# A two-block float32 model on one core: late projection tiles of the mixers in three split products, and another order of work in the first blocks

## The reference

```
for l in range(2):
    x = x + 0.5 * swiglu(rms_norm(x, ffn1_norm[l]), ffn1_w_gate_up[l], ffn1_w_down[l])
    u = rms_norm(x, mix_norm[l]) @ w_in[l]
    u_ssd, u_ml, u_rw = jnp.split(u, [D_SSD_IN, D_SSD_IN + D_MLSTM_IN], axis=-1)
    y = jnp.concatenate([ssd_mixer(u_ssd, ...), mlstm_mixer(u_ml, ...), rwkv7_mixer(u_rw, ...)], axis=-1)
    x = x + y @ w_out[l]
    x = x + 0.5 * swiglu(rms_norm(x, ffn2_norm[l]), ffn2_w_gate_up[l], ffn2_w_down[l])
x = rms_norm(x, final_norm)
mod = silu(c) @ w_ada + b_ada          # then the second block: attention, convolution, FFN
```

## Time and profile before

| | us |
|---|---|
| median of 3 runs | 1765.9 |
| lowest, highest | 1763.33, 1766.49 |
| the profiled execution | 1766.17 |
| its span in the trace | 1764.3 |
| TensorE busy | 1714.5 (97%) |
| VectorE busy | 1290.3 (73%) |
| ScalarE busy | 931.6 (53%) |
| GpSimd busy | 406.9 (23%) |

### The profile page before, as it was taken

How to read it: one execution, slowest core, us unless ns; L and a number is a source line. 1 busy time by engine, 2 the same in 40 slices (tenths; PEclk the granted TensorE clock), 3 DMA queues, 4 the chain that set the end, 5 groups by cost and what they waited for, 6 DMA issues and landing times.

```text
span 1764.3 us, 32985 instructions
## 1 busy us (share of the span) xinstructions
PE 1714.5 (97%) x13956; PEld 1550.1 (88%) x13956; DVE 1290.3 (73%) x2141; ACT 931.6 (53%) x1666; POOL 406.9 (23%) x316
## 2 busy tenths in 40 slices
PE   7999999999899999999999999989999999999997
PEld 6888998888898888888899888889888898999987
DVE  5887775865667887688777586575887675789974
ACT  5774536323446764577443632344676546557652
POOL 2772000000213761167100000021466100111110
PEclk9999999999999999999999999999999999999999
DMA  7675622211146665566562221105575553345543
GB/s 255 238 280 185 220 105 96 87 53 39 43 168 258 237 227 184 212 253 228 185 217 96 96 97 50 50 26 191 215 257 190 198 176 124 108 145 190 176 149 106
DMA packets 45059, 282.70 MB, mean 160 GB/s; under 512 B 6128, under 2 KB 6768, under 8 KB 18544
## 3 DMA queue, kind: packets, MB, share of 16 engines
q1 hardware_dynamic: 44912, 280.60, 44.5%
HBM read 279.53 MB, written 1.05 MB: 159 GB/s over the span
## 4 chain that ended last, share of the span: by engine, by line
PE 85%; DVE 9%; ACT 4%; issue 1%; DMA 1%; POOL 0%; SPq 0%; DVEq 0%; ACTq 0%
PE banks L531 27%; PE banks L532 14%; PE banks L1071 8%; PE banks L523 7%; PE banks L524 7%; PE banks L525 7%; PE banks L1680 3%; DVE WL L494 2%; PE banks L563 1%; ACT WH L489 1%; PE banks L1949 1%; DMA ring<-wst 1%; PE banks L1959 0%; PE banks L743 0%; PE banks L1213 0%
## 5 line engine op out<-in xcount | busy, mean ns | idle before, releaser
L494 DVE TENSOR_TENSOR WL<-ring,WH 128x2048 fp32r<-128x2048 f32 (+1 forms) x219 | 459.7, 2110 | 111.0 <-ACT WH L489 110.8
L531 PE MATMUL banks<-XNP,WH 128*128 128x512 f32 x1408 | 498.7, 399 | 10.7 <-DVE XNP L621 8.5
L489 ACT ACTIVATE WH<-ring 128x2048 fp32r<-128x2048 f32 (+1 forms) x223 | 380.8, 1716 | 52.9 <-PE banks L525 46.1
L532 PE MATMUL banks<-XNP,WL 128*128 128x256 f32 x1408 | 393.3, 279 | 0.0
L531 PEld LDWEIGHTS banks<-XNP,WH 128*128 128x128 f32 x1408 | 266.1, 189 | 72.8 <-DVE XNP L621 9.0
L969 POOL TENSOR_TENSOR HP<-G,HP 128x256 fp32r<-128x256 f32 x110 | 210.2, 1912 | 309.9 <-ACT HP L781 309.9
L531 PE MATMUL banks<-HP,WH 128*128 128x512 f32 x770 | 267.5, 392 | 0.8 <-POOL HP L969 0.7
L532 PEld LDWEIGHTS banks<-XNP,WL 128*128 128x128 f32 x1408 | 266.6, 189 | 0.0
L532 PE MATMUL banks<-HP,WL 128*128 128x256 f32 x770 | 215.2, 280 | 0.0
L1071 PE MATMUL banks<-XN,ring 128*128 128x256 f32 x832 | 191.7, 381 | 0.0
L531 PEld LDWEIGHTS banks<-HP,WH 128*128 128x128 f32 x770 | 144.5, 188 | 33.3 <-POOL HP L969 1.4
(11 more groups left out here) (498 smaller groups left out, 3311.8 us busy)
## 6 DMA issues: line engine op xcount, KB each, us to landing
ring<-wst SPq DMA_DIRECT2D x205, 1024.0 KB, 4.8
ring<-wst SPq DMA_DIRECT2D x80, 704.0 KB, 4.1
LP<-lp SPq DMA_DIRECT2D x1, 1872.0 KB, 8.7
LP<-lp SPq DMA_DIRECT2D x4, 448.0 KB, 5.6
ring<-wst SPq DMA_DIRECT2D x2, 512.0 KB, 5.5
X<-xin SPq DMA_DIRECT2D x2, 512.0 KB, 6.3
out<-X SPq DMA_DIRECT2D x4, 256.0 KB, 2.6
C<-cst SPq DMA_DIRECT2D x1, 193.0 KB, 4.9
```

The lines of the kernel that those rows point to most:

```text
L489: e.do.activation(WH[:, slot[q], 0:n], ring[:, i % NSLOT, 0:n], ACT.Copy).then_inc(*w_act.up("high", q))
L494: e.do.tensor_tensor(WL[:, slot[q], 0:n], ring[:, i % NSLOT, 0:n], WH[:, slot[q], 0:n].bitcast(F32), ALU.subtract).then_inc(*w_dve.up("low ...
L531: e.do.matmul(b[:, :], WH[:, s, cols], x.rearrange("p s t -> p (s t)"), start=first, stop=False)
L532: return e.do.matmul(b[:, 0:T], WL[:, s, cols], x[:, 0, :], start=False, stop=last)
```

## The change

**Late tiles.** The 26 late tiles are cut into 52 half units u, each of four contraction steps of one tile. SyncE loads a half unit in a transfer of its own (128 x 4 x 128, 256 KB), as soon as half u-8 has been multiplied, into a quarter of one of two ring slots. The third slot of the ring takes the high parts of four half units: `act_late_high` on ScalarE (128x512) at the step three half steps ahead of TensorE's. `dve_late_low` on VectorE (128x512) replaces the block by its low part in place, two half steps ahead. The first four of them come at every second half step before. XN is split too: its high parts go to room that isn't in use then (`xh_late`: parts of `G2`, `LP`, `AL` and `GAP`), by eight instructions of ScalarE at the tiles 7 to 13; its low parts replace XN, by eight of VectorE at the tiles 9, 10, 11 and 13. TensorE does 12 fp32r products for a half unit instead of four plain ones. Because `AL` is used so, its load is moved behind the second layer's tiles (semaphore `s_al`); the first blocks of `w_out` go to the ring after half 47 or 51. The table `order_of` isn't touched.

**First blocks.** TensorE begins with ten plain products on a buffer of ones (`pe_begin`), ahead of any data. LP's load goes before that of X. Block 1 is split in halves like block 0, and TensorE takes both column halves h of a contraction step in turn in the pairs j = 0 and 1. The squares go to eight buffers in place of two; GpSimd adds only the first four, and TensorE adds the rest in `pe_first_sums`. The modulation blocks of the first FFN stand after the pairs 7, 10, 13, 16, 19 and 21.

```diff
-ADA_UP = (5, 8, 11, 14, 17, 20)
+def ada_up(f):
+    return (7, 10, 13, 16, 19, 21) if f == 0 else (5, 8, 11, 14, 17, 20)
...
+        def slot_freed(i):
+            name, l, what = plan[i]
+            if name == "w_out" and what[1] < NSLOT:
+                return p_pe.on("half", l, 47 if what[1] == 0 else 51)
+            return freed(holds[item[i] - NSLOT])
...
+        def pe_begin(e):
+            e.wait_ge(*in_dve.on("warm"))
+            for _ in range(10):
+                m = e.do.matmul(bank[7][:, 0:T], ACC[:, 0:128], ACC[:, :], start=True, stop=True)
+            m.then_inc(*in_pe.up("warm"))
...
+            for half in range(2):
+                at = slice(1024 * half, 1024 * half + 1024)
+                e.wait_ge(*landed(1))
+                e.do.activation(WH[:, 1, at], ring[:, 1, at], ACT.Copy).then_inc(*(w_act.up("high", 1) if half else w_act.up("high half", 1)))
             for n in range(KT):
-                if n >= 2:
-                    e.wait_ge(*in_pool.on("sum", n - 2))
-                e.do.activation(SQ[:, n % 2, :], X[:, n, :], ACT.Square).then_inc(*in_act.up("sq", n))
-                if n in (1, 4):
-                    act_high(e, n // 3 + 1)
+                e.do.activation(squares[n], X[:, n, :], ACT.Square).then_inc(*in_act.up("sq", n))
+            act_high(e, 2)
...
+            e.wait_ge(*in_pe.on("warm"))
+            e.wait_ge(*in_act.on("sq", 1))
+            e.do.tensor_tensor(ACC[:, :], squares[0], squares[1], ALU.add).then_inc(*in_pool.up("sum", 1))
+            for n in (2, 3):
                 e.wait_ge(*in_act.on("sq", n))
-                pool_sum(e, in_pool, n, ("sum", n))
+                e.wait_ge(*in_pool.last())
+                e.do.tensor_tensor(ACC[:, :], ACC[:, :], squares[n], ALU.add).then_inc(*in_pool.up("sum", n))
...
+        def pe_first_sums(e):
+            parts = [ACC[:, :], *squares[4:]]
+            for c in range(2):
+                for i, q in enumerate(parts):
+                    m = e.do.matmul(bank[6][:, c:c + 1], q[:, c * 128:c * 128 + 128], ones[:, 0:1], start=i == 0, stop=i == 4)
+            m.then_inc(*f_pe.up("sums", 0))
...
-                for h in range(2):
-                    for k in range(KT):
+                early = f == 0 and j < 2
+                for h, k in ((i % 2, i // 2) if early else (i // KT, i % KT) for i in range(2 * KT)):
                         if j + h == 0:
                             e.wait_ge(*x_low_on(f, k))
-                            if f == 0:
-                                e.wait_ge(*(w_dve.on("first half") if k < 4 else low_on(q)))
+                        if early:
+                            e.wait_ge(*(w_dve.on("low half", q) if k < 4 else low_on(q)))
...
+        xh_late = [G2r[:, i, 1, :] for i in range(3)] + [LPr[:, LC["wig"] + T * i:LC["wig"] + T * i + T] for i in range(2)] + [
+            ALr[:, 0:T]] + [GAPr[:, T * i:T * i + T] for i in range(2)]
+        def late_slot(l, n):
+            return slot_at(place["w_in", l, ("two", EARLY - 3 + n)])
+        def late_weights(of, l, u):
+            return of[:, late_slot(l, u % 8 // 4), 512 * (u % 4):512 * (u % 4) + 512]
+        def late_high(l, u):
+            return ringr[:, late_slot(l, 2), 512 * (u % 4):512 * (u % 4) + 512]
+        def late_at(step, ahead):
+            u = step + ahead - 4 * EARLY
+            if u < 4:
+                return u // 2 + 3 if u in (-6, -4, -2, 0) else None
+            return u if u < 52 else None
+        def act_late_high(e, l, u):
+            if u is None:
+                return
+            e.wait_ge(*(p_pe.on("half", l, u - 4) if u >= 4 else freed(place["w_in", l, ("two", EARLY - 1)])))
+            e.wait_ge(s_late[u % 8], 16 * (u // 8 + 1 + (l * (7 if u % 8 < 4 else 6))))
+            e.do.activation(late_high(l, u), late_weights(ring, l, u), ACT.Copy).then_inc(*w_act.up("late high", l, u))
+        def dve_late_low(e, l, u):
+            if u is None:
+                return
+            e.wait_ge(*w_act.on("late high", l, u))
+            e.do.tensor_tensor(late_weights(ringr, l, u), late_weights(ring, l, u), late_high(l, u).bitcast(F32), ALU.subtract).then_inc(
+                *w_dve.up("late low", l, u))
+        def act_x_high(e, l, k):
+            e.wait_ge(*p_dve.on("normed", l, k // 4 * 4))
+            if k >= 6:
+                e.wait_ge(*p_pe.on("tile", l, 2 * EARLY - 1))
+            e.do.activation(xh_late[k], XN[:, k, :], ACT.Copy).then_inc(*p_act.up("xh", l, k))
+        def dve_x_low(e, l, k):
+            e.wait_ge(*p_act.on("xh", l, k))
+            e.wait_ge(*s_pe.on("gates", l))
+            e.do.tensor_tensor(XNr[:, k, :], XN[:, k, :], xh_late[k].bitcast(F32), ALU.subtract).then_inc(*p_dve.up("xl", l, k))
...
-                                wt = ring[:, place["w_in", l, ("two", n)] % NSLOT, :]
-                                m = e.do.matmul(b[:, 0:T], wt[:, at], XN[:, kt, :], start=kt == 0, stop=kt == KT - 1)
-                        if half:
+                                u = 2 * (i - 2 * EARLY) + half
+                                e.wait_ge(*w_dve.on("late low", l, u))
+                                if i == 2 * EARLY:
+                                    e.wait_ge(*p_act.on("xh", l, kt))
+                                    e.wait_ge(*p_dve.on("xl", l, kt))
+                                at = slice((kt - 4 * half) * 128, (kt - 4 * half) * 128 + 128)
+                                wl, wh = late_weights(ringr, l, u)[:, at], late_high(l, u)[:, at]
+                                e.do.matmul(b[:, 0:T], wh, xh_late[kt], start=kt == 0, stop=False)
+                                e.do.matmul(b[:, 0:T], wh, XNr[:, kt, :], start=False, stop=False)
+                                m = e.do.matmul(b[:, 0:T], wl, xh_late[kt], start=False, stop=kt == KT - 1)
+                        if i >= 2 * EARLY:
+                            m.then_inc(*(p_pe.up("half", l, 2 * (i - 2 * EARLY) + half)))
+                            if half:
+                                p_pe.at["tile", l, i] = p_pe.n
...
         def act_proj(e, l):
             for i in range(43):
-                yield
+                act_late_high(e, l, late_at(2 * i, 3))
+                yield
+                act_late_high(e, l, late_at(2 * i + 1, 3))
...
+                if 7 <= i < 13:
+                    act_x_high(e, l, i - 7)
+                if i == 13:
+                    act_x_high(e, l, 6)
+                    act_x_high(e, l, 7)
...
+                dve_late_low(e, l, late_at(2 * i, 2))
...
+                if 9 <= i < 12:
+                    dve_x_low(e, l, 2 * i - 18)
+                    dve_x_low(e, l, 2 * i - 17)
+                if i == 13:
+                    dve_x_low(e, l, 6)
+                    dve_x_low(e, l, 7)
+                dve_late_low(e, l, late_at(2 * i + 1, 2))
...
+                if by_tiles(name, what):
+                    both = wst[i].rearrange("p (k s t) -> p k s t", k=KT, s=2)
+                    for p in range(4):
+                        u = 4 * (what[1] - EARLY) + p
+                        e.wait_ge(*(p_pe.on("half", l, u - 8) if u >= 8 else freed(place["w_in", l, ("two", EARLY - 3 + u // 4)])))
+                        e.do.dma_start(late_weights(ring, l, u).rearrange("p (k t) -> p k t", k=4),
+                                       both[:, 4 * (p % 2):4 * (p % 2) + 4, p // 2, :]).then_inc(s_late[u % 8], 16)
```

103 lines of the change are left out of this document (68 added, 35 removed).

## The result

| kernel | median us | runs | ratio to before | 95% interval |
|---|---|---|---|---|
| before | 1765.6 | 9 | | |
| changed | 1772.33 | 9 | 1.0042 | 1.0031 to 1.0053 |

The changed kernel is slower by 0.4%, 6.7 us; 1770 was forecast. Its profiled execution took 1769.63 us (span 1767.8), one of the faster of its nine, which go from 1768.51 to 1778.48. Before they went from 1763.03 to 1766.49. That the runs spread three times as far has to do with the clock of TensorE, see experiment 5.

A forecast was written before the change was run, and what follows sets the result against it. VectorE, without room in the mixers' middle stretch, was taken to bind there, rather than TensorE with its 97%. 1766.17 - 6.2 (opening) + 2 x (2.2 mixers + 2.7 clock) = 1769.8, about 1770; range 1750 to 1781.

The forecast's parts named there:

- rival B: Mixers: TensorE stays the bound, VectorE takes in the lows, all 31 us show: 1729; chance 0.10.
- Tile 14: First layer, about 254.1 us: TensorE waits about 1.8 us at contraction step 6 for the last X lows.
- A: Layer length from the last split tile to the middle stretch (252 to 289.5 us): ends 0.4 us later.
- B: Middle stretch, 289.5 to 345.1 us: 20 lows exceed VectorE's usable idle time, +7.1 us.
- C: Layer length from the middle stretch to its end (345.1 to 438.6 us): 3.8 gained, leaving +2.2 per layer.
- The clock: Mixers: new TensorE waits bring the clock to 0.50, costing 2.7 us per layer, 1.0 at 255 and 1.7 at 305.
- The opening: First blocks, up to about 60 us: warm-up and moved modulation block, -6.2 us in all, between -3.5 and -7.0.
- -2.3 from the warm-up: Opening: warm-up products absorb TensorE's slow first pace; block 0 could end 2.85 us earlier, 0.55 held back: -2.3.
- -3.9 at the modulation block: First FFN: moving the block from j=5 to j=7 removes two waits and a cold stretch, 4.7; -3.9 kept.
- its half: Rival B': middle stretch costs +4.9, outer stretches keep their 9.6 us per layer: 1751; chance 0.13.
- D: Rival: mixers come out even, -1 to +1 each, VectorE's idle time taking more lows: 1758 to 1763; chance 0.15.
- C's mechanism: Rival C: clock falls repeatedly in the middle stretch, another 3.4 to 6.8 us a layer, 1776 to 1785; chance 0.17.

The follow-up runs named there:

- experiment 5: Test of what lost clock costs: the changed kernel with products by a zero matrix in seven TensorE waits per layer; 1769.98 us, ratio 1.0022 to before.
- the fill: Zero-matrix products keeping TensorE busy in seven mixer waits per layer, added to the changed kernel (the run of experiment 5); 1769.98 us, ratio 1.0022.
- high 12 earlier: Changed kernel with the high part of half 12 ahead of ScalarE's series of gates instead of behind it; 1778.99 us, ratio 1.0073 to before.
- the fills at the lanes: First blocks' part alone, mixers as before, with 3 and 5 plain products in two TensorE waits per layer ahead of a cold stretch; 1757.9 us, ratio 0.9956.

## Why the prediction was right, and where its terms were off

**What bounds.** That the chain through VectorE, and not TensorE with its 97%, sets the middle stretch: shown, by the lows left out. By the rule behind rival B 1729 would have come; the row of 25.10 in 25.8 us was the better guide.

**TensorE's saving.** 0.30 us per half: the 12 products' pace is as forecast, 0.36 for three. TensorE's busy time sank by 17 us only, since 7.5 us of warm-up products (20 records from 1.2 us on) and more stretches at the slow clock are in it.

**Tile 14.** Forecast a wait of 1.8; it is 2.36, in both layers.

**A.** Forecast +0.4; it is +1.3 and +1.7. The scans behind half 12's high: forecast start about 277.1 in the old count; it is 274.46, and 5.0 later in that count, 279.5.

**B.** Forecast +7.1; it is +7.2 in both layers. L1930 is 8.5 us later against the first tiles where 7.5 was forecast. The waits of 1.9, 2.6, 2.0, 2.6 and 2.8 us are 1.11, 2.38, 1.77, 2.44 and 2.50. The walk along both orders with the durations of the rows gave this number; no mean of busy times does. The prediction gives of that walk only these five waits and its end.

**C.** The forecast had L1799 7.5 us later and the layer's end 2.2, so -5.3 in this count; it is -3.1 and -4.8. In the first layer a cold stretch (392.2) lies in it.

**The clock.** Forecast 2.7 per layer on top; the fill gives 3.5 for both layers, 1.8 per layer. I put 1.7 of it at 305, in the middle stretch, but what fell there in the changed kernel's profile fell at 331 and cost nothing. A fall at 305 came with high 12 earlier, and cost 2.6. Size about right, place wrong, and by luck in part. The sum per layer, forecast 4.9, is 5.4 and 4.1 in the profiled execution, and 6.4 by the late tiles' part alone. In these measured lengths the clock's share is inside A and C, where the forecast had it beside them: A and C without it were forecast too short, and the clock's term made up for that.

**The opening.** Forecast -6.2; it is -5.0 in the profiled execution and -4.2 by medians. Here the single terms were wrong. The step "-2.3 from the warm-up" failed: measured 0. "-3.9 at the modulation block" is 5.0 on TensorE at the ninth pair (58.77 against 63.76, one modulation block behind it in both). Its reason, three sums of GpSimd in place of seven, wasn't needed: with seven the moved block meets no wait either. But of this gain only part outlives the FFN, unless the first stage's edits bring VectorE forward by 2 us; I had not followed VectorE's lag to the end of the FFN. That TensorE was busy for 87.00 of 87.00 us showed me that nothing waits in between, not that nothing waits behind.

**The sum.** 1769.8 against 1772.33. The mixers cost up to 3 us more than forecast and the opening brings 2 less than forecast, both in the same direction. Against the change itself the miss isn't small: +3.6 was forecast and +6.7 came. 1770 looks near because all terms are small beside 1770, and the time of one profiled execution (1769.63) is nearer than a median over runs that the clock spreads.

**Rivals.** B (1729) and its half (1751) are excluded: the middle can't give its 6.0. D (mixers even) is excluded by the late tiles' part alone, 12.9 us over before. C's mechanism, the clock falling again and again, is there in part: the profiled execution of that part alone, with one fall more in B of the first layer, took 1781.3, and the changed kernel's runs reach up to 1778, into C's range.

## What to carry to other kernels

Before making the busiest engine's work cheaper by giving work to another, take the stretch in which the other is fullest and walk both queues through it; with a busy share in the nineties on both, one of them may only be filling, as TensorE was here. A gain on an engine that is ahead of its suppliers arrives where the supplier is late, which can be 100 us further on. A cold stretch of TensorE's clock is worth chasing only where TensorE has the path; keeping it busy in the waits ahead, with products into a free bank, removed the falls at 471 and 1174 us, but not the one at 1526.

## What was not expected of the hardware

- VectorE's operations with two SBUF operands stood still while GpSimd's 128x512 subtraction ran: 1.49 us in place of 0.41. One with a single SBUF operand did too (1.38 in place of 0.28), and those that read PSUM didn't.
- A cold stretch of 6.8 us in the middle stretch cost 2.6 us where VectorE was half idle, and 0.0 where VectorE was full.
- With 9.7 us of lost clock won back only 3.5 us came in, though run by run each lost us went with 0.90 us of time. In the kernel with the fills at the lanes the loss is 9.2 us of clock, against 14.8 in the runs before beside it, and its four runs lie within 0.44 us.
- Warm-up products ahead of the first real one brought TensorE's first pair from a pace of 0.64 us per step to 0.35, as meant, and the time didn't move.
- A cold stretch of 3.4 us follows the small one-column products near 24 us in the profiled executions of the first blocks' part alone and of the kernel without the middle's lows, but not in that of the changed kernel, whose program up to there is the same. The fall isn't a matter of the program alone.
